# Recurrence gates activated by ScalarE straight from PSUM in the input projection, with their logarithms and scans moved there

## Chip, core and metric

The kernel runs on one core of a Trainium2 chip. The metric is device time in microseconds (us) for one execution of the whole program. The kernel before takes 2365.54 us, the median of three runs (2364.43 to 2369.72).

## What is computed

Two transformer blocks on one sequence of 512 tokens, width 1024, all in float32. The change lies in the first part of the first block, which mixes tokens in two ways from one projection:

```
proj = rmsnorm(h) @ w_in           # 512 x 3592
fq, fk, fv, ff, gq, gf, gi, gg = split(proj)   # widths 512,512,512,8,512,512,512,512
log_f = log_sigmoid(ff + bias)
fox   = softmax(fq fk^T/8 + F[t] - F[s], causal) fv      # F = cumsum(log_f), 8 heads of 64
f  = lb + (1 - lb) * sigmoid(gf);  k = 1 - f;  g = log(f)
q  = silu(gq)
S_t = diag(f_t) S_{t-1} + k_t i_t^T;  rec_t = S_t^T q_t      # 4 heads of 128, in chunks
rec = rmsnorm(rec) * silu(gg)
h  = h + concat(fox, rec) @ w_out
```

The recurrence needs, besides q, k and i, the cumulative sums of g within chunks. After it follow cross attention, a feed-forward part, and the second block; the change touches nothing there.

## The kernel before

Activations lie transposed in SBUF (features on 128 partitions, 512 tokens along the free dimension) unless noted. The program is written by hand for five instruction streams (TensorE, VectorE, ScalarE, GpSimd which the profile calls POOL, and SyncE for the DMAs), which meet through counting semaphores. Each engine works through its own stream in order, so a wait in one stream holds all that stands behind it there.

**Weights.** `plan` cuts every weight matrix into units of 1024 x 256 (1 MB). For each unit SyncE loads `raw`, ScalarE copies it to the rounded high part `wH` (L635, helper `high`), and POOL subtracts to give the low part `wL` (L511, helper `low`). There are two buffers of each. TensorE multiplies high by high, low by high and high by low (L1701 to L1703), so a unit is two blocks of 24 matmuls of 128x512 (feature units), or two blocks of token-major output (token units). `high(n)` waits until unit n - 2 is used up. TensorE waits for both parts of a unit.

**PSUM.** Block b goes to bank b % 4. Before a block TensorE waits until block b - 4 is taken out: `bank_free` looks at `BY_ACT` to see whether that was VectorE's work (semaphore `blk_taken`, counts in `TAKEN`) or ScalarE's (`silu_done`, counts in `SILUS`). In the kernel before only the `ffn_w1` units of the second block are ScalarE's.

**The input projection** has 15 units: 0 to 5 for fq, fk, fv, unit 6 (one block, the eight forget logits), 7 and 8 for gq, 9 and 10 for gf (tile `gk`), 11 and 12 for gi (token units), 13 and 14 for gg. VectorE takes each block from PSUM with a copy (helper `take`, L1084). ScalarE's stream here is `high(n + 1)` for each unit, and at unit 8 the three operations of the forget rows (L750 to L752: Abs, Exp, Ln), after which VectorE forms the cumulative sums `frow` (L1182 to L1184) between the blocks of gk and gi.

**The first attention** (`attention("fox")`) starts when all blocks are taken. It has 8 heads of 4 query blocks, so 32 steps s. TensorE: in step s the scores (L1805) and the causal mask (L1807), the transposes of step s - 3 (L1854), and after a head's last step its eight value matmuls (L1832); once a head, a broadcast of the next head's forget sums (L1796). VectorE: maximum with subtraction (L1112), then the reciprocal and scaling of the step before (L1121, L1122). ScalarE: exponential (L705), the copy of the transposed weights (L724), the broadcast's copy (L694), once per two heads the high part of the output (L730). All depend on each other within a few steps.

Into this chain the kernel before lays the gates of the recurrence. At step 8 ScalarE applies Silu to all of `gq`, Silu to all of `gg` and Sigmoid to all of `gk` (128x2048 each, L710 to L712). From step 10 on VectorE takes one item of `gate_steps` per step: a mask (L1193, L1194), then for each of four heads f and k = 1 - f (L1198, L1199); at step 16 ScalarE takes the logarithms (L716), six steps later VectorE runs the four scans (L1205). The recurrence's own stage begins after the attention on all engines.

A function of ScalarE that is not in the table at hand brings a table load; it appears as ACT_TABLE_LOAD under the line that needs it.

Of the kernel before, what the change touches and what calls it, by code (L numbers as in the profile page):

```python
# [11 lines left out]
ALU = mybir.AluOpType  # L12
ACT = mybir.ActivationFunctionType
# [97 lines left out]
N_UNITS = len(UNITS)  # L111
BLOCK0 = [sum(u[5] for u in UNITS[:n]) for n in range(N_UNITS + 1)]

BY_ACT = [u[0].startswith("ffn_w1") for u in UNITS for _ in range(u[5])]
TAKEN = [sum(not x for x in BY_ACT[:b]) for b in range(len(BY_ACT) + 1)]
SILUS = [sum(x for x in BY_ACT[:b]) for b in range(len(BY_ACT) + 1)]

# [64 lines left out]
def bass_block_pair(nc, a, out):  # L182
# [155 lines left out]
    with ExitStack() as ctx:  # L338
# [25 lines left out]
        f_l, f_rows, f_bc, f_bcs = sem("f_l"), sem("f_rows"), sem("f_bc"), sem("f_bcs")  # L364

        lvl_in = sem("lvl_in")
        h_act, h_fk, h_ln, h_b = sem("h_act"), sem("h_fk"), sem("h_ln"), sem("h_b")
        h_d, h_e, h_q, h_k, h_pl, h_at = sem("h_d"), sem("h_e"), sem("h_q"), sem("h_k"), sem("h_pl"), sem("h_at")
        h_eb, h_qb, h_kd, h_kt, h_kts, h_sp, h_st, h_o, h_os = (
            sem("h_eb"), sem("h_qb"), sem("h_kd"), sem("h_kt"), sem("h_kts"), sem("h_sp"), sem("h_st"), sem("h_o"), sem("h_os"))  # L370
# [246 lines left out]
        def _(act):  # L617
# [63 lines left out]
            def attention(kind):  # L681
                c = ATT[kind]
                ns = c["heads"] * TB
                width = {"fox": None, "cross": M_MEM, "grid": S}[kind]
                for s in range(ns + 7):
                    g = c["step0"] + s
                    if kind == "fox":

                        h = 0 if s == 0 else (s + 2) // 4 if s % 4 == 2 else FOX_H
                        if h < FOX_H:  # L690
                            act.wait_ge(f_bc, h + 1)
                            if h >= 2:
                                act.wait_ge(mx_done, 4 * (h - 1))
                            nc.scalar.activation(fbc[h % 2][:], ps[2 + h % 2][:], ACT.Copy).then_inc(f_bcs, 1)  # L694
                    if s < ns:
                        i = s % TB
                        w = (i + 1) * P if kind == "fox" else width
                        act.wait_ge(mx_done, g + 1)
                        if kind == "fox":
                            src = pr[g % PR_RING][:, 0:w]  # L700
                        else:
                            src = ps[4 + g % 2][:, 0:w]
                            act.wait_ge(tp_done, g - PR_RING + 1)
                        m = g % PR_RING
                        nc.scalar.activation(pr[m][:, 0:w], src, ACT.Exp, bias=nmax[:, m:m + 1],  # L705
                                             accum_out=rsum[:, m:m + 1]).then_inc(ex_done, 1)
                    if kind == "fox" and s == 8:

                        act.wait_ge(blk_taken, TAKEN[BLOCK0[AT["out"][0]]])
                        nc.scalar.activation(gq[:], gq[:], ACT.Silu).then_inc(h_act, 1)  # L710
                        nc.scalar.activation(gg[:], gg[:], ACT.Silu).then_inc(h_act, 1)
                        nc.scalar.activation(gk[:], gk[:], ACT.Sigmoid).then_inc(h_act, 1)  # L712
                    if kind == "fox" and s == 16:
                        for hh in range(HG_H):
                            act.wait_ge(h_fk, hh + 1)
                            nc.scalar.activation(lnf[:, hh, :], lnf[:, hh, :], ACT.Ln).then_inc(h_ln, 1)  # L716
                    t = s - 3
                    if 0 <= t < ns:
                        h, i = t // TB, t % TB
                        nj = (i + 1) if kind == "fox" else width // P  # L720
                        act.wait_ge(tp_done, c["step0"] + t + 1)
                        if i == 0 and h >= 2:
                            act.wait_ge(pv_done, c["pv0"] + c["pvh"] * (h - 1))
                        nc.scalar.activation(pT[h % 2][:, 0:nj, i * P:(i + 1) * P],  # L724
                                             ps[6 + (c["step0"] + t) % 2][:, 0:nj * P].rearrange("p (j t) -> p j t", j=nj),
                                             ACT.Copy).then_inc(pt_done, 1)

                    for o in outputs(kind, s - 5):
                        act.wait_ge(pv_done, c["pv0"] + (o + 1 if kind == "cross" else 2 * o + 2))
                        nc.scalar.activation(uH[:, c["col0"] + o, :], ps[o % 2][:], ACT.Copy).then_inc(op_hi, 1)  # L730
# [13 lines left out]
            nc.scalar.activation(lbt[:, 8:16], lbt[:, 0:8], ACT.Exp).then_inc(setup, 1)  # L744
            for u, n in enumerate(range(*ranges("in"))):
                high(n + 1)
                if u == 8:

                    act.wait_ge(blk_taken, TAKEN[BLOCK0[AT["in"][0]] + 13])
                    chain(nc.scalar.activation(frow[1][:], fz[:], ACT.Abs))  # L750
# [241 lines left out]
        def _(dve):  # L992
# [104 lines left out]
            def attention(kind):  # L1097
# [3 lines left out]
                for s in range(ns + 8):  # L1101
# [15 lines left out]
                    if 1 <= s <= ns:  # L1117
# [2 lines left out]
                        dve.wait_ge(ex_done, g)  # L1120
                        chain(nc.vector.reciprocal(rinv[:, m:m + 1], rsum[:, m:m + 1]))  # L1121
                        nc.vector.tensor_scalar(pr[m][:, 0:w], pr[m][:, 0:w], rinv[:, m:m + 1], None, ALU.mult).then_inc(pn_done, 1)  # L1122
                    if kind == "fox" and s >= 10:
                        next(hgrn_gates, None)
                    for o in outputs(kind, s - 6):
                        low_op(c["q0"] + o, uL[:, c["col0"] + o, :], ps[o % 2][:], uH[:, c["col0"] + o, :])

# [45 lines left out]
            fb = b + 12  # L1173
            dve.wait_ge(blk_done, fb + 1)
            nc.vector.tensor_scalar(fz[:], ps[fb % 4][0:FOX_H, :], fbias[0:FOX_H, :], None, ALU.add).then_inc(blk_taken, 1)
            for j in range(4):
                take(fb + 1 + j, gq[:, j, :], ps[(fb + 1 + j) % 4][:])
            for j in range(4):
                take(fb + 5 + j, gk[:, j, :], ps[(fb + 5 + j) % 4][:])

            dve.wait_ge(f_l, 1)
            chain(nc.vector.tensor_scalar(frow[2][:], fz[:], 0.0, None, ALU.min))  # L1182
            chain(nc.vector.tensor_tensor(frow[2][:], frow[2][:], frow[1][:], ALU.subtract))
            nc.vector.tensor_tensor_scan(frow[0][:], ones[0:FOX_H, 0:1].to_broadcast([FOX_H, S]), frow[2][:], 0.0,  # L1184
                                         ALU.mult, ALU.add).then_inc(f_rows, 1)
            for u in range(2):
                take_tokens(fb + 9 + 2 * u, gi, u * UC)
            for j in range(4):
                take(fb + 13 + j, gg[:, j, :], ps[(fb + 13 + j) % 4][:])


            def gate_steps():
                chain(nc.vector.memset(rmask[:], 1.0))  # L1193
                chain(nc.vector.memset(rmask[:].rearrange("p (c t) -> p c t", c=TB)[:, :, 0:1], 0.0))  # L1194
                yield
                dve.wait_ge(h_act, 3)
                for h in range(HG_H):
                    chain(nc.vector.tensor_scalar(lnf[:, h, :], gk[:, h, :], omlb[:, h:h + 1], lb[:, h:h + 1], ALU.mult, ALU.add))  # L1198
                    nc.vector.tensor_scalar(gk[:, h, :], lnf[:, h, :], -1.0, 1.0, ALU.mult, ALU.add).then_inc(h_fk, 1)  # L1199
                    yield  # L1200
                for _ in range(6):
                    yield
                for h in range(HG_H):
                    dve.wait_ge(h_ln, h + 1)
                    nc.vector.tensor_tensor_scan(gb[:, h, :], rmask[:], lnf[:, h, :], 0.0, ALU.mult, ALU.add).then_inc(h_b, 1)  # L1205
                    yield

            hgrn_gates = gate_steps()
            attention("fox")
            for _ in hgrn_gates:  # L1210
                pass

            levels = [(h, l) for h in range(HG_H) for l in range(len(HG_LEVELS))]

# [473 lines left out]
        def _(pe):  # L1688
# [98 lines left out]
            def attention(kind):  # L1787
                c = ATT[kind]
                ns = c["heads"] * TB
                pe.wait_ge(blk_taken, TAKEN[BLOCK0[AT[{"fox": "out", "cross": "xo", "grid": "ev_out"}[kind]][0]]])  # L1790

                def gates_everywhere(h):

# [441 lines left out]
```

## Time and profile before

| What | Value |
|---|---|
| median of three runs | 2365.54 us (2364.43 to 2369.72) |
| the profiled execution, its own time | 2369.94 us |
| its span, first to last instruction | 2368.2 us |
| TensorE matmuls busy | 2172.1 us, 92% |
| VectorE busy | 1148.0 us, 48% |
| ScalarE busy | 705.6 us, 30% |
| POOL busy | 845.1 us, 36% |
| mean granted TensorE clock | 0.947 |

All rows come from one execution. Times count from the span's start. PE is TensorE, PEld its weight loads, DVE VectorE, ACT ScalarE. The granted clock is a share of 2.4 GHz: 1.00 is full, 0.50 is half. In a timeline, `[6.21 <-ACT pT L724]` means that the engine was idle for 6.21 us before and was released by that instruction. Matmuls are pipelined, so the durations of neighbours overlap. The profiled execution is one, and the three runs spread over 5 us, so a difference of one or two microseconds between two profiles says little.

### The profile page before, as it was taken

Reading aid. Unit: us, or ns where it says so; the run is one execution under the profiler, and the core shown is the slowest. Engines: PE = TensorE matmul, PEld = TensorE weight load, DVE = VectorE, ACT = ScalarE, POOL = GpSimd, SP = SyncE. Lnnn points to the kernel's source line nnn. Section 1 sums busy time; section 2 is a strip of 40 time slices with the busy share of each in tenths; the row PEclk is TensorE's granted clock in tenths of the full one; section 3 lists DMA queues with packets and bytes.
Section 4 is the critical chain, followed back from the end, with each engine's and each line's share of the span. In section 5 each row is a group of like instructions: output and inputs, shape, how many; then the busy total and the mean of one; then the engine's idle time right before and its main releaser. Section 6 shows DMA issues by size and latency. Waiting matters only on the chain.

```text
span 2368.2 us, 26471 instructions
## 1 busy us (share of the span) xinstructions
PE 2172.1 (92%) x10170; PEld 1730.1 (73%) x10170; DVE 1148.0 (48%) x1876; ACT 705.6 (30%) x938; POOL 845.1 (36%) x303
## 2 busy tenths in 40 slices
PE   6998866899989999989988999999899878999998
PEld 4884355787768788877347888888798557888887
DVE  4112597553378888453545676632465554111112
ACT  3124522332331322333433212222233333222221
POOL 2441063362333333423203443334343323434342
PEclk8997868999999999989899999999999989999999
DMA  4330000342245554222004555522222002232322
GB/s 135 96 92 0 1 10 21 105 143 72 90 142 185 177 191 137 89 71 103 0 18 142 178 178 177 193 91 89 89 90 72 1 1 89 89 107 89 106 85 76
DMA packets 220414, 226.12 MB, mean 95 GB/s; under 512 B 3787, under 2 KB 218524, under 8 KB 220188
## 3 DMA queue, kind: packets, MB, share of 16 engines
q1 hardware_dynamic: 220316, 224.78, 29.2%
q8 instruction: 65, 1.06, 0.2%
q14 instruction: 33, 0.27, 0.0%
HBM read 222.67 MB, written 2.10 MB: 95 GB/s over the span
## 4 chain that ended last, share of the span: by engine, by line
PE 79%; DVE 8%; issue 6%; ACT 4%; POOL 1%; DMA 1%; SPq 0%; DVEq 0%; ACTq 0%; POOLq 0%
PE ps L1701 23%; PE ps L1703 22%; PE ps L1702 22%; PE ps L1832 2%; PE ps L1812 1%; DVE adacc L1379 1%; PE ps L1854 1%; PE ps L1916 1%; ACT wH L635 1%; PE ps L1805 1%; PE ps L1768 1%; PE ps L1823 1%; DVE T L1062 1%; DVE uL L1047 1%; DVE hnL L1049 0%
## 5 line engine op out<-in xcount | busy, mean ns | idle before, releaser
L511 POOL TENSOR_TENSOR wL<-raw,wH 128x2048 fp32r<-128x2048 f32 (+2 forms) x161 | 729.8, 4534 | 1274.6 <-ACT wH L635 1259.9
L1701 PE MATMUL ps<-hnH,wH 128*128 128x512 f32 x1336 | 529.5, 396 | 27.1 <-DVE hnL L1049 14.4
L1703 PE MATMUL ps<-hnH,wL 128*128 128x512 f32 x1336 | 524.5, 393 | 0.0
L1702 PE MATMUL ps<-hnL,wH 128*128 128x512 f32 x1336 | 524.0, 392 | 0.0
L635 ACT ACTIVATE wH<-raw 128x2048 fp32r<-128x2048 f32 (+2 forms) x161 | 302.4, 1879 | 651.1 <-PE ps L1703 631.8
L1701 PE MATMUL ps<-uH,wH 128*128 128x512 f32 x864 | 341.3, 395 | 14.2 <-DVE uL L1047 9.7
L1703 PE MATMUL ps<-uH,wL 128*128 128x512 f32 x864 | 338.6, 392 | 0.0
L1702 PE MATMUL ps<-uL,wH 128*128 128x512 f32 x864 | 338.0, 391 | 0.0
L1701 PEld LDWEIGHTS ps<-hnH,wH 128*128 128x128 f32 x1336 | 253.9, 190 | 81.7 <-issue 30.1
L1703 PEld LDWEIGHTS ps<-hnH,wL 128*128 128x128 f32 x1336 | 253.3, 190 | 53.8
L1702 PEld LDWEIGHTS ps<-hnL,wH 128*128 128x128 f32 x1336 | 254.0, 190 | 52.5 <-issue 0.5
L1379 DVE SCALAR_TENSOR_TENSOR adacc<-adaw,small,adacc 128x256 f32<-128x256 f32 x336 | 278.9, 830 | 12.0
L1701 PEld LDWEIGHTS ps<-uH,wH 128*128 128x128 f32 x864 | 163.5, 189 | 49.8 <-issue 13.5
L1703 PEld LDWEIGHTS ps<-uH,wL 128*128 128x128 f32 x864 | 163.2, 189 | 34.5
L1702 PEld LDWEIGHTS ps<-uL,wH 128*128 128x128 f32 x864 | 163.4, 189 | 33.4
L1505 DVE TENSOR_TENSOR T<-ps,R 128x512 f32<-128x512 f32 x44 | 30.4, 691 | 323.7 <-PE ps L1703 323.7
L1094 DVE SCALAR_TENSOR_TENSOR xT<-ps,mod,xT 128x512 f32<-128x512 f32 x64 | 47.5, 750 | 192.5 <-PE ps L1703 192.4
L1701 PE MATMUL ps<-wH,hnH 128*128 128x256 f32 (+1 forms) x416 | 117.8, 283 | 2.9 <-issue 2.9
L1702 PE MATMUL ps<-wL,hnH 128*128 128x256 f32 (+1 forms) x416 | 117.5, 282 | 0.0
L1703 PE MATMUL ps<-wH,hnL 128*128 128x256 f32 (+1 forms) x416 | 117.5, 282 | 0.0
L1408 DVE TENSOR_TENSOR uL<-T,uH 128x512 fp32r<-128x512 f32 x32 | 84.6, 2681 | 21.7 <-ACT uH L834 21.7
L898 ACT ACTIVATE uH<-T 128x512 fp32r<-128x512 f32 x44 | 27.8, 633 | 190.6 <-DVE T L1505 190.6
(331 smaller groups left out, 2506.8 us busy)
## 6 DMA issues: line engine op xcount, KB each, us to landing
raw<-in_ffn_w_dram SPq DMA_DIRECT2D x60, 1024.0 KB, 5.3
adaw<-in_ada_w_dram SPq DMA_DIRECT2D x48, 1024.0 KB, 7.3
raw<-in_w_dram SPq DMA_DIRECT2D x32, 1024.0 KB, 5.4
raw<-in_w_in_dram SPq DMA_DIRECT2D x14, 1024.0 KB, 5.4
raw<-in_od_w_in_dram SPq DMA_DIRECT2D x12, 1024.0 KB, 5.3
raw<-in_w_xkv_dram SPq DMA_DIRECT2D x8, 1024.0 KB, 5.3
raw<-in_ffn_w_dram SPq DMA_DIRECT2D x8, 768.0 KB, 4.2
raw<-in_ev_w_in_dram SPq DMA_DIRECT2D x5, 1024.0 KB, 5.4
```

The lines of the kernel that those rows point to most:

```text
L511: nc.gpsimd.tensor_tensor(wL[n % 2][:, 0:kc, 0:c], raw[n % 2][:, 0:kc, 0:c], wH[n % 2][:, 0:kc, 0:c].bitcast(F32), ALU.subtract).then_inc( ...
L635: nc.scalar.activation(wH[n % 2][:, 0:kc, 0:c], raw[n % 2][:, 0:kc, 0:c], ACT.Copy).then_inc(w_hi, 1)
L898: nc.scalar.activation(uH[:, 2 * p + c, :], T[(q0 + c) % 2][:], ACT.Copy).then_inc(op_hi, 1)
L1047: nc.vector.tensor_tensor(dstL, src, dstH.bitcast(F32), ALU.subtract).then_inc(op_lo, 1)
L1094: nc.vector.scalar_tensor_tensor(out=xT[:, j, :], in0=ps[b % 4][:], scalar=gate(j), in1=xT[:, j, :], op0=ALU.mult, op1=ALU.add).then_inc(b ...
L1379: ins = nc.vector.scalar_tensor_tensor(out=acc, in0=adaw[m % ADA_RING][:, k, :], scalar=condc[:, k:k + 1], in1=acc, op0=ALU.mult, op1=ALU.add)
L1408: nc.vector.tensor_tensor(uL[:, 2 * u + c, :], T[q % 2][:], uH[:, 2 * u + c, :].bitcast(F32), ALU.subtract).then_inc(op_lo, 1)
L1505: nc.vector.tensor_tensor(T[(q0 + c) % 2][:], ps[b % 4][:], R[c][:], ALU.mult).then_inc(blk_taken, 1)
L1701: nc.tensor.matmul(out_ap, wh, xh, start=first, stop=False)
L1702: nc.tensor.matmul(out_ap, wh, xl, start=False, stop=False)
L1703: return nc.tensor.matmul(out_ap, wl, xh, start=False, stop=last)
L1832: ins = nc.tensor.matmul(ps[h // 2 % 2][hp:hp + 64, t0:S], v, pT[h % 2][:, j, t0:S], start=(j == 0), stop=(j == TB - 1))
```

## The change

The blocks of units 7 to 10, 13 and 14 become ScalarE's: as each of the twelve is finished in PSUM, ScalarE applies Silu (gq, gg) or Sigmoid (gk) from the bank into SBUF, in place of VectorE's copy, and counts `silu_done`. In ScalarE's stream the two activations of a unit stand behind `high(n + 1)` of the same unit. The forget rows' three operations move from unit 8 to unit 11, the four logarithms from the attention's step 16 to unit 12. VectorE forms f and k head by head as the blocks of gk are activated, takes the first half of gi, then forms the forget sums, takes the second half of gi, and runs the four scans, all before the attention. The attention's streams lose all of this; TensorE now waits at its start for `silu_done` as well.

```diff
--- before.py
+++ after.py
@@ -111,7 +111,8 @@
 N_UNITS = len(UNITS)
 BLOCK0 = [sum(u[5] for u in UNITS[:n]) for n in range(N_UNITS + 1)]
 
-BY_ACT = [u[0].startswith("ffn_w1") for u in UNITS for _ in range(u[5])]
+GATE_UNITS = (7, 8, 9, 10, 13, 14)
+BY_ACT = [u[0].startswith("ffn_w1") or n in GATE_UNITS for n, u in enumerate(UNITS) for _ in range(u[5])]
 TAKEN = [sum(not x for x in BY_ACT[:b]) for b in range(len(BY_ACT) + 1)]
 SILUS = [sum(x for x in BY_ACT[:b]) for b in range(len(BY_ACT) + 1)]
 
@@ -364,7 +365,7 @@
         f_l, f_rows, f_bc, f_bcs = sem("f_l"), sem("f_rows"), sem("f_bc"), sem("f_bcs")
 
         lvl_in = sem("lvl_in")
-        h_act, h_fk, h_ln, h_b = sem("h_act"), sem("h_fk"), sem("h_ln"), sem("h_b")
+        h_fk, h_ln, h_b = sem("h_fk"), sem("h_ln"), sem("h_b")
         h_d, h_e, h_q, h_k, h_pl, h_at = sem("h_d"), sem("h_e"), sem("h_q"), sem("h_k"), sem("h_pl"), sem("h_at")
         h_eb, h_qb, h_kd, h_kt, h_kts, h_sp, h_st, h_o, h_os = (
             sem("h_eb"), sem("h_qb"), sem("h_kd"), sem("h_kt"), sem("h_kts"), sem("h_sp"), sem("h_st"), sem("h_o"), sem("h_os"))
@@ -704,16 +705,6 @@
                         m = g % PR_RING
                         nc.scalar.activation(pr[m][:, 0:w], src, ACT.Exp, bias=nmax[:, m:m + 1],
                                              accum_out=rsum[:, m:m + 1]).then_inc(ex_done, 1)
-                    if kind == "fox" and s == 8:
-
-                        act.wait_ge(blk_taken, TAKEN[BLOCK0[AT["out"][0]]])
-                        nc.scalar.activation(gq[:], gq[:], ACT.Silu).then_inc(h_act, 1)
-                        nc.scalar.activation(gg[:], gg[:], ACT.Silu).then_inc(h_act, 1)
-                        nc.scalar.activation(gk[:], gk[:], ACT.Sigmoid).then_inc(h_act, 1)
-                    if kind == "fox" and s == 16:
-                        for hh in range(HG_H):
-                            act.wait_ge(h_fk, hh + 1)
-                            nc.scalar.activation(lnf[:, hh, :], lnf[:, hh, :], ACT.Ln).then_inc(h_ln, 1)
                     t = s - 3
                     if 0 <= t < ns:
                         h, i = t // TB, t % TB
@@ -744,7 +735,17 @@
             nc.scalar.activation(lbt[:, 8:16], lbt[:, 0:8], ACT.Exp).then_inc(setup, 1)
             for u, n in enumerate(range(*ranges("in"))):
                 high(n + 1)
-                if u == 8:
+                if u in GATE_UNITS:
+                    dst, func = {7: (gq, ACT.Silu), 9: (gk, ACT.Sigmoid), 13: (gg, ACT.Silu)}[u - (u + 1) % 2]
+                    for c in range(2):
+                        b = BLOCK0[n] + c
+                        act.wait_ge(blk_done, b + 1)
+                        nc.scalar.activation(dst[:, 2 * ((u + 1) % 2) + c, :], ps[b % 4][:], func).then_inc(silu_done, 1)
+                if u == 12:
+                    for hh in range(HG_H):
+                        act.wait_ge(h_fk, hh + 1)
+                        nc.scalar.activation(lnf[:, hh, :], lnf[:, hh, :], ACT.Ln).then_inc(h_ln, 1)
+                if u == 11:
 
                     act.wait_ge(blk_taken, TAKEN[BLOCK0[AT["in"][0]] + 13])
                     chain(nc.scalar.activation(frow[1][:], fz[:], ACT.Abs))
@@ -1120,8 +1121,6 @@
                         dve.wait_ge(ex_done, g)
                         chain(nc.vector.reciprocal(rinv[:, m:m + 1], rsum[:, m:m + 1]))
                         nc.vector.tensor_scalar(pr[m][:, 0:w], pr[m][:, 0:w], rinv[:, m:m + 1], None, ALU.mult).then_inc(pn_done, 1)
-                    if kind == "fox" and s >= 10:
-                        next(hgrn_gates, None)
                     for o in outputs(kind, s - 6):
                         low_op(c["q0"] + o, uL[:, c["col0"] + o, :], ps[o % 2][:], uH[:, c["col0"] + o, :])
 
@@ -1173,42 +1172,24 @@
             fb = b + 12
             dve.wait_ge(blk_done, fb + 1)
             nc.vector.tensor_scalar(fz[:], ps[fb % 4][0:FOX_H, :], fbias[0:FOX_H, :], None, ALU.add).then_inc(blk_taken, 1)
-            for j in range(4):
-                take(fb + 1 + j, gq[:, j, :], ps[(fb + 1 + j) % 4][:])
-            for j in range(4):
-                take(fb + 5 + j, gk[:, j, :], ps[(fb + 5 + j) % 4][:])
-
+            chain(nc.vector.memset(rmask[:], 1.0))
+            chain(nc.vector.memset(rmask[:].rearrange("p (c t) -> p c t", c=TB)[:, :, 0:1], 0.0))
+            for h in range(HG_H):
+                dve.wait_ge(silu_done, SILUS[fb + 5 + h + 1])
+                chain(nc.vector.tensor_scalar(lnf[:, h, :], gk[:, h, :], omlb[:, h:h + 1], lb[:, h:h + 1], ALU.mult, ALU.add))
+                nc.vector.tensor_scalar(gk[:, h, :], lnf[:, h, :], -1.0, 1.0, ALU.mult, ALU.add).then_inc(h_fk, 1)
+            take_tokens(fb + 9, gi, 0)
             dve.wait_ge(f_l, 1)
             chain(nc.vector.tensor_scalar(frow[2][:], fz[:], 0.0, None, ALU.min))
             chain(nc.vector.tensor_tensor(frow[2][:], frow[2][:], frow[1][:], ALU.subtract))
             nc.vector.tensor_tensor_scan(frow[0][:], ones[0:FOX_H, 0:1].to_broadcast([FOX_H, S]), frow[2][:], 0.0,
                                          ALU.mult, ALU.add).then_inc(f_rows, 1)
-            for u in range(2):
-                take_tokens(fb + 9 + 2 * u, gi, u * UC)
-            for j in range(4):
-                take(fb + 13 + j, gg[:, j, :], ps[(fb + 13 + j) % 4][:])
-
-
-            def gate_steps():
-                chain(nc.vector.memset(rmask[:], 1.0))
-                chain(nc.vector.memset(rmask[:].rearrange("p (c t) -> p c t", c=TB)[:, :, 0:1], 0.0))
-                yield
-                dve.wait_ge(h_act, 3)
-                for h in range(HG_H):
-                    chain(nc.vector.tensor_scalar(lnf[:, h, :], gk[:, h, :], omlb[:, h:h + 1], lb[:, h:h + 1], ALU.mult, ALU.add))
-                    nc.vector.tensor_scalar(gk[:, h, :], lnf[:, h, :], -1.0, 1.0, ALU.mult, ALU.add).then_inc(h_fk, 1)
-                    yield
-                for _ in range(6):
-                    yield
-                for h in range(HG_H):
-                    dve.wait_ge(h_ln, h + 1)
-                    nc.vector.tensor_tensor_scan(gb[:, h, :], rmask[:], lnf[:, h, :], 0.0, ALU.mult, ALU.add).then_inc(h_b, 1)
-                    yield
-
-            hgrn_gates = gate_steps()
+            take_tokens(fb + 11, gi, UC)
+            for h in range(HG_H):
+                dve.wait_ge(h_ln, h + 1)
+                nc.vector.tensor_tensor_scan(gb[:, h, :], rmask[:], lnf[:, h, :], 0.0, ALU.mult, ALU.add).then_inc(h_b, 1)
             attention("fox")
-            for _ in hgrn_gates:
-                pass
+            dve.wait_ge(silu_done, SILUS[BLOCK0[AT["out"][0]]])
 
             levels = [(h, l) for h in range(HG_H) for l in range(len(HG_LEVELS))]
 
@@ -1788,6 +1769,8 @@
                 c = ATT[kind]
                 ns = c["heads"] * TB
                 pe.wait_ge(blk_taken, TAKEN[BLOCK0[AT[{"fox": "out", "cross": "xo", "grid": "ev_out"}[kind]][0]]])
+                if kind == "fox":
+                    pe.wait_ge(silu_done, SILUS[BLOCK0[AT["out"][0]]])
 
                 def gates_everywhere(h):
```

## Rows read from the trace of the kernel before

**Rows 1.** The page: the chain that ended last, by line

```profile
PE ps L1701 23%; PE ps L1703 22%; PE ps L1702 22%; PE ps L1832 2%; PE ps L1812 1%; DVE adacc L1379 1%; PE ps L1854 1%; PE ps L1916 1%; ACT wH L635 1%; PE ps L1805 1%; PE ps L1768 1%; PE ps L1823 1%; DVE T L1062 1%; DVE uL L1047 1%; DVE hnL L1049 0%
```

**Rows 2.** Busy time by stretch: us, PE, PEld, DVE, ACT, POOL, clock, DMA share, GB/s

```profile
85.00:198.00 113.00, 111.19 (x647) 98.31 (x646) 16.43 (x24) 21.46 (x14) 45.36 (x11) 1.00 0.28 84
198.00:296.00 98.00, 85.36 (x256) 35.56 (x256) 46.41 (x180) 52.68 (x121) 0.00 (x0) 0.74 0.00 1
```

**Rows 3.** ScalarE groups of the attention: count, busy us, mean ns, idle before

```profile
L705 ACT ACT_TABLE_LOAD x3 | 3.8, 1283 | 0.1
...
L716 ACT ACTIVATE lnf<-lnf 128x512 f32<-128x512 f32 x4 | 2.2, 616 | 0.0
...
L710 ACT ACTIVATE gq<-gq 128x2048 f32<-128x2048 f32 x1 | 1.9, 1910 | 0.0
```

**Rows 4.** Timeline of TensorE, waits for ScalarE: start, duration, [idle before, releaser]

```profile
231.82 1.09 PE L1854 MATMUL ps<-cst,pr 128*128 128x128 f32 x4 [6.21 <-ACT pT L724]
...
254.60 1.08 PE L1854 MATMUL ps<-cst,pr 128*128 128x128 f32 x4 [1.25 <-ACT pT L724]
```

**Rows 5.** Busy time of the attention, cut where the clock changes

```profile
198.30:221.20 22.90, 22.90 (x49) 8.64 (x49) 8.28 (x38) 9.48 (x25) 0.00 (x0) 0.57 0.00 0
221.20:225.20 4.00, 4.00 (x16) 1.93 (x15) 1.93 (x10) 2.50 (x4) 0.00 (x0) 0.93 0.00 0
...
238.90:252.50 13.60, 12.21 (x51) 5.62 (x49) 9.21 (x37) 7.16 (x18) 0.00 (x0) 1.00 0.00 1
...
262.70:266.10 3.40, 3.40 (x15) 1.72 (x15) 1.52 (x9) 1.25 (x4) 0.00 (x0) 1.00 0.00 0
266.10:272.90 6.80, 6.80 (x14) 2.20 (x13) 6.62 (x17) 3.63 (x10) 0.00 (x0) 0.50 0.01 2
272.90:295.90 23.00, 20.07 (x85) 9.48 (x83) 11.65 (x46) 10.66 (x30) 0.00 (x0) 1.00 0.00 0
```

**Rows 6.** Timeline of TensorE: first score matmuls of heads, and value matmuls

```profile
206.29 0.79 PE L1805 MATMUL ps<-fk,fq 64*128 64x128 f32 x2
...
216.76 4.53 PE L1832 MATMUL ps<-pT,fv 128*64 128x512 f32 x8
221.22 0.73 PE L1805 MATMUL ps<-fk,fq 64*128 64x128 f32 x2
...
239.47 0.48 PE L1805 MATMUL ps<-fk,fq 64*128 64x128 f32 x2
...
248.99 0.49 PE L1805 MATMUL ps<-fk,fq 64*128 64x128 f32 x2
...
270.54 3.55 PE L1832 MATMUL ps<-pT,fv 128*64 128x512 f32 x8
274.02 0.49 PE L1805 MATMUL ps<-fk,fq 64*128 64x128 f32 x2
...
282.43 0.49 PE L1805 MATMUL ps<-fk,fq 64*128 64x128 f32 x2
```

**Rows 7.** VectorE groups of the gate steps, 230 to 280 us

```profile
L1205 DVE TENSOR_TENSOR_SCAN gb<-rmask,lnf 128x512 f32<-128x512 f32 x4 | 4.9, 1217 | 0.0
...
L1198 DVE TENSOR_SCALAR lnf<-gk,small 128x512 f32<-128x512 f32 x4 | 2.2, 541 | 0.0
...
L1199 DVE TENSOR_SCALAR gk<-lnf 128x512 f32<-128x512 f32 x4 | 1.7, 427 | 0.1
```

**Rows 8.** ScalarE groups of the whole span: Silu from PSUM in a later stage

```profile
L894 ACT ACTIVATE R<-ps 128x512 f32<-128x512 f32 x44 | 25.9, 598 | 133.5 <-PE ps L1703 133.5
```

**Rows 9.** Timeline of ScalarE, then of POOL: the weights' high and low parts

```profile
141.90 1.92 ACT L635 ACTIVATE wH<-raw 128x2048 fp32r<-128x2048 f32 x1 [8.96 <-PE ps L1703]
152.78 1.91 ACT L635 ACTIVATE wH<-raw 128x2048 fp32r<-128x2048 f32 x1 [8.96 <-PE ps L1703]
...
143.89 4.60 POOL L511 TENSOR_TENSOR wL<-raw,wH 128x2048 fp32r<-128x2048 f32 x1 [6.28 <-ACT wH L635]
154.77 5.35 POOL L511 TENSOR_TENSOR wL<-raw,wH 128x2048 fp32r<-128x2048 f32 x1 [6.28 <-ACT wH L635]
```

## The prediction

> **What bounds the kernel now.** I read the page's chain first: three lines of weight-block matmuls hold 67% of it [rows 1]. Work moved from one helper engine to another can matter only where TensorE waits for it, so the next view is the busy time by stretch around the diff [rows 2]. The input projection, to 198 us, has TensorE at 111 of 113 us and full clock, with VectorE and ScalarE busy for 16 and 21 us. The first attention, 198 to 296 us, has TensorE at 85 of 98 us, a mean clock of 0.74, ScalarE at 53, VectorE at 46 and POOL at 0.
>
> Third, the ScalarE groups of the attention [rows 3], one row for each pattern: Silu on 128x2048 takes 1.91 us (a second Silu and the Sigmoid the same), a logarithm 0.62 us, a table load 1.28 us. Fourth, TensorE's waits for ScalarE there [rows 4]: transposes that wait 6.21 us until 231.82, since ScalarE is at the activations, and 1.25 us until 254.60, at the logarithms. Fifth, the stage cut where the granted clock changes [rows 5]: full (2.4 GHz) for 4.0, 13.6, 3.4 and 23.0 us, half (1.2 GHz) for nearly all the rest, some 54 us.
>
> The clock matters as much as the waits. The first score matmuls of two consecutive heads stand at 206.29 and 221.22, a head at half clock, 14.9 us; later at 274.02 and 282.43, a head at full clock, 8.4 us, one scan in it [rows 6]. The rises at 221.2 and 272.9 lie in or right behind a head's eight value matmuls (from 216.76, from 270.54), and so do the two between them. The falls at 225.2 and 266.1 come with TensorE busy for 4.00 of 4.00 and 3.40 of 3.40 us since the rise [rows 5], in the sparse steps behind such a run; that at 252.5 comes before the second wait begins (254.60 - 1.25 = 253.35).
>
> **The change part by part.** *Activations in the attention, removed.* ScalarE loses three of 1.9 us, four logarithms (2.5 us) and five table loads: one each for Silu, Sigmoid and Ln, two that bring Exp back (L705's third, at the attention's start, stays), 6.4 us [rows 3]. Of these 14.6 us TensorE felt 6.2 + 1.25 us as waits [rows 4].
>
> *VectorE's gate steps in the attention, removed.* Four pairs of 0.54 and 0.43 us and four scans of 1.22 us, 8.8 us [rows 7]. The head from 239.47 to 248.99 ran at full clock with three of the pairs in it and took 9.5 us against 8.4 us [rows 6]: 1.1 us on the path. Two of the scans lie in the half-clock stretch in which TensorE was busy 6.80 of 6.80 us [rows 5]: hidden.
>
> *The clock.* From the first step of head 2 (221.22) to that of head 7 (282.43) are five heads in 61.2 us [rows 6]. Five at the full-clock price are 42.0 us, 19.2 us less. That is the most; it takes in the waits and steps above. But the fall at 225.2 came before ScalarE's absence reached TensorE (231.82 - 6.21 = 225.6) [rows 4, 5], so nothing in the change removes it. It catches the head about half way, and the half clock then lasts into that head's value matmuls, as before. One such spell costs half of a head's difference, (14.9 - 8.4) / 2 = 3.3 us; with a small chance of a second I take 3.5 us (0 and 3 x 3.5 are the ends). The start to 221.2 and the end from 282.43 on hold nothing of the change. **Sum for the attention: 19.2 - 3.5 = 15.7 us.**
>
> The rows thus show falls with a busy engine. The Trainium skill ("TensorE: Matmul & The Clock Gate", section "Why this matters for your kernels") lays drops in mid-kernel to idle gaps between bursts of matmuls; by it no fall would be left once both waits are gone, and the sum would be 19.2 us. The trace disagrees for the falls named.
>
> *Twelve activations from PSUM, added to ScalarE in the projection.* Silu of a 128x512 bank takes 0.60 us [rows 8], in place of a VectorE copy. Each pair is followed on ScalarE by the high part of a coming unit's weights, and that by POOL's low part, for which TensorE waits. Today the high part starts when a unit ends (141.90, 152.78: a unit lasts 10.9 us) and the low part, from 143.89 on, is done after 4.60 us, 6.6 us behind the start: 4.3 us of cover [rows 9]. A unit's second activation comes first now and takes 0.65 us of it. Table loads are issued while ScalarE idles between blocks. Cost nothing; without the cover, 0.65 us for each of six units, 3.9 us.
>
> *The forget gate's three operations* move behind the high part at 152.78, with one more table load: some 4.5 us, ready near 160. VectorE asks for them a unit on, near 165; the row sums are used at 198. The logarithms come behind the next high part and end near 169, the scans run from 176 on. Cost nothing, 20 us of cover. A gate block's PSUM bank is asked for some three blocks, 16 us, after its activation: nothing. SP and POOL keep their order and no DMA is moved.
>
> *VectorE's pairs and scans in the projection* run beside POOL's subtraction; in the attention POOL was idle [rows 2]. The subtraction at 154.77, with the forget rows' sum in its time, took 5.35 instead of 4.60 us [rows 9]. Four scans in a row could add four times that, 3 us, against 4.3 - 0.65 us of cover. 0 to 1 us on the path, 0 taken, as the cover is larger.
>
> *The attention's start.* TensorE waits for a 0.60 us activation of the last bank instead of a copy; ScalarE loads Exp behind its first copy, as now. Between a gain of 0.1 and a loss of 1.3 us (a load in the way); 0 taken, since the load keeps its place.
>
> **Sum against the profiled execution:** 2369.9 - 15.7 = 2354.2 us. That execution is 4.4 us above the median of the three runs. If those 4.4 us lie elsewhere, the new median is 2349.8; if in this attention, 2354.2. I take 2351, nearer to the first, since the stage is only 98 of 2368 us.
>
> **The rivals.** *A, the clock stays up.* No fall after 221.2: 19.2 us, 2350.7 on the profiled basis, 2346 as a median. For it: 23.0 us at full clock at the stage's end [rows 5]. Against: the two falls with a busy engine.
>
> *B, only the waits go.* The clock falls as often as today and the change gives back 6.2 + 1.3 + 1.1 + some 0.3 us for a scan, 8.9 us: 2361.0, or 2356.6 as a median. For it: falls came behind value matmuls without any of the gates' work. Against: heads that follow each other more densely should lose the clock less often.
>
> *C, POOL's weights come late.* With scans and a pair beside it the subtraction outgrows its cover and TensorE waits 1 to 4 us before the last units: 2352 to 2355. For it the 5.35 us row, against it the cover. The Trainium skill ("GPSIMD Engine Reference", Specifications) has POOL's SBUF interface shared with VectorE instructions of two SBUF inputs or in a two-port mode, which speaks against moving these twelve steps here; the row agrees, its size stays inside the cover.
>
> *D, slower: the clock never comes back in this stage.* Five heads at half clock take 5 x 14.9 = 74.5 us for today's 61.2, and the last 13.5 us some 7 more: 20 us slower, 2386 as a median. Each head at half costs 6.5 of the 19.2 us: from three on the gain is gone, from four on it is a loss above 0.2%. Against: each of the four value runs that met half clock brought it back.
>
> *E, no effect:* the removed work lay beside the chain. The 6.21 us wait speaks against it.
>
> **How the numbers follow.** Forecast 0.52, A 0.17, B 0.20, C 0.04, E 0.04, D 0.03. The range goes from A with 3 us for the luck of single runs, 2343, to B with its 4.4 us above, 2361; E, D and a rest of the others lie outside, under 0.2. A measurement of this kernel can tell some 0.2%, 4.7 us, from no change. Faster 0.93, same 0.04, slower 0.03.
>
> **What would show it.** In the changed profile: no table load between the attention's first exponential and its end; no TensorE wait above 2 us for a ScalarE copy there; the stage some 82 us long (79 by A, 89 by B, 118 by D); POOL's subtractions ended 3 us before the unit that needs them, TensorE above 98% busy in the projection; and the first fall of the clock again before 226 us. A projection over 1 us longer makes the second part wrong, a stage of 89 us or more the third.

## The result, and the profile after

The changed kernel takes 2352.26 us (median; 2346.77 to 2355.88, five runs) against 2365.54 us before: a ratio of 0.9937 [0.9925, 0.995], 13.3 us less. A second series of the same kernel, called c_change below, gave 2346.86 us (2346.22 to 2351.37) against 2368.46: 0.9918 [0.9904, 0.9931], 21.6 us less. Of the 8.3 us between the two gains, 5.4 are the changed kernel's and 2.9 those of the kernel before, whose medians differ too. The ten runs together have a median of 2350.2 us, and they spread over 9.7 us, which is itself a finding (below).

I cut each profiled execution at the first broadcast matmul of the attention, at VectorE's first operation of the recurrence behind it, and at the first matmul of the output projection. In us:

| kernel | start and projection | attention | recurrence | rest | span |
|---|---|---|---|---|---|
| before | 198.3 | 97.7 | 114.0 | 1958.2 | 2368.2 |
| changed, first series | 199.5 | 85.9 | 113.9 | 1954.8 | 2354.1 |
| changed, c_change | 198.5 | 77.5 | 114.6 | 1954.4 | 2345.1 |

So 11.8 us of the 14.1 come from the attention in the one profile, and 20.1 of 23.1 in the other. Some 3.5 us come in both from behind the recurrence, where the diff touches nothing. (In the first profile everything from the high part at 58.70 us on, at 57.44 before, is some 1.2 us late; that stands in the set-up.)

The page of the changed kernel, its chain by line, beside [rows 1]; its large terms are where they were:

```profile
PE ps L1682 23%; PE ps L1684 23%; PE ps L1683 23%; PE ps L1815 2%; PE ps L1795 1%; PE ps L1788 1%; PE ps L1837 1%; DVE adacc L1360 1%; PE ps L1899 1%; PE ps L1749 1%; ACT wH L636 1%; PE ps L1806 1%; DVE uL L1048 1%; DVE at L1227 0%; PE ps L2102 0%
```

Busy time by stretch of the changed kernel, first series, columns as in [rows 2] (us, PE, PEld, DVE, ACT, POOL, clock, DMA share, GB/s):

```profile
85.00:199.30 114.30, 112.45 (x658) 99.61 (x656) 23.19 (x26) 35.20 (x34) 47.31 (x11) 1.00 0.27 83
199.30:285.50 86.20, 82.45 (x256) 34.54 (x256) 37.81 (x165) 38.80 (x110) 0.00 (x0) 0.78 0.00 1
```

and the same of c_change:

```profile
85.00:198.40 113.40, 111.47 (x650) 98.59 (x648) 23.19 (x26) 35.29 (x34) 46.34 (x11) 1.00 0.28 84
198.40:276.00 77.60, 73.02 (x256) 31.67 (x256) 37.59 (x164) 38.73 (x110) 0.00 (x0) 0.89 0.00 1
```

ScalarE's 52.7 us in the attention are 38.8 and VectorE's 46.4 are 37.8; what is missing stands in the projection now. TensorE issues the same 256 matmuls. In both profiles it idles less, 12.6 us before, 3.8 and 4.6 now. What differs between the two is the clock, 0.78 and 0.89. The first attention cut where the clock changes, first series, beside [rows 5]:

```profile
221.20:224.80 3.60, 3.60 (x15) 1.68 (x15) 1.84 (x10) 1.01 (x4) 0.00 (x0) 0.97 0.00 0
224.80:231.60 6.80, 6.80 (x14) 2.44 (x14) 2.60 (x11) 3.38 (x10) 0.00 (x0) 0.51 0.00 0
231.60:245.20 13.60, 13.12 (x57) 6.18 (x55) 7.05 (x32) 6.46 (x20) 0.00 (x0) 1.00 0.00 1
245.20:252.00 6.80, 6.80 (x14) 2.31 (x13) 2.34 (x10) 2.80 (x8) 0.00 (x0) 0.50 0.00 0
252.00:255.60 3.60, 3.60 (x17) 1.85 (x16) 1.58 (x9) 1.25 (x4) 0.00 (x0) 0.97 0.00 0
255.60:262.40 6.80, 6.80 (x14) 2.21 (x13) 3.46 (x14) 3.63 (x10) 0.00 (x0) 0.51 0.01 2
262.40:285.40 23.00, 20.02 (x85) 9.47 (x83) 10.58 (x45) 10.70 (x30) 0.00 (x0) 1.00 0.00 0
```

and c_change's:

```profile
198.50:202.20 3.70, 3.69 (x11) 1.60 (x12) 0.59 (x4) 2.37 (x4) 0.00 (x0) 0.99 0.00 0
202.20:219.20 17.00, 17.00 (x35) 6.23 (x35) 7.69 (x35) 7.10 (x21) 0.00 (x0) 0.50 0.00 1
219.20:276.00 56.80, 52.33 (x212) 23.83 (x210) 29.30 (x126) 29.24 (x84) 0.00 (x0) 1.00 0.00 1
```

The same program had three spells at half clock behind the first rise in one execution, and none in the other. All three begin with TensorE at work since the rise: busy for 3.60 of 3.60, 13.12 of 13.60 and 3.60 of 3.60 us.

The waits of [rows 4] are gone. So is a third, of 1.40 us until 246.69, in the head that had three of VectorE's pairs in it (the two operations for f and k). ScalarE loads one table in this stage where it loaded six. TensorE's longest wait for ScalarE there, from the timeline of the first series, is the ordinary one for a head's last exponential:

```profile
281.75 2.37 PE L1815 MATMUL ps<-pT,fv 128*64 128x512 f32 x8 [0.69 <-ACT pT L715]
```

### The profile page after: what moved, and what is told of

It is laid out like the page before. It is cut to its first block, busy times and chain, and to the rows that moved or that the text cites. A ratio compares the mean times of both kernels' runs of the same rounds, so it can differ in the third digit from the quotient of the medians.

```text
span 2354.1 us, 26492 instructions
## 1 busy us (share of the span) xinstructions
PE 2169.4 (92%) x10170; PEld 1730.1 (73%) x10170; DVE 1141.3 (48%) x1864; ACT 705.6 (30%) x946; POOL 845.9 (36%) x303
## 4 chain that ended last, share of the span: by engine, by line
PE 81%; DVE 8%; issue 6%; ACT 2%; POOL 1%; DMA 0%; DVEq 0%; SPq 0%; ACTq 0%; POOLq 0%
PE ps L1682 23%; PE ps L1684 23%; PE ps L1683 23%; PE ps L1815 2%; PE ps L1795 1%; PE ps L1788 1%; PE ps L1837 1%; DVE adacc L1360 1%; PE ps L1899 1%; PE ps L1749 1%; ACT wH L636 1%; PE ps L1806 1%; DVE uL L1048 1%; DVE at L1227 0%; PE ps L2102 0%
```

## The experiments

Ten kernels ran, in three series with their own runs of the kernel before, whose medians are 2368.46, 2367.28 and 2367.68 us; so a difference of one microsecond between kernels of two series says nothing. "Wide" marks those with e3's broadcast. Each kernel has one profile, and a stage's length in one profile holds what the clock did in it. A spell is a stretch at half clock.

**c_change: the same kernel again.**

> The change as it is, again, so that the others of this call have it on the same chip. All theories: 2350 to 2354 us as a median, 11 to 15 us under the kernel before. The stage of the first attention is 86 us long in the change's profile and 98 us in the profile of before; since the times of single runs spread over 9 us, another profile should show another number of stretches at half clock in that stage (the change's first had three after 221 us), and the stage's length should follow it by some 3 us for each.

Measured: 2346.86 us, 3 us below what I expected, with the attention at 77.5 us. Five heads took 42.4 us from one score matmul (220.12) to another (262.55); the forecast's full-clock price was 42.0. In the first series the same five took 50.8 us with three spells: 8.4 us more, 2.8 us for each.

**e1_acts_only: only the twelve activations are moved.** Logarithms, pairs and scans go back into the attention:

```
+    if kind == "fox" and s == 16:
+        for hh in range(HG_H):
+            act.wait_ge(h_fk, hh + 1)
+            nc.scalar.activation(lnf[:, hh, :], lnf[:, hh, :], ACT.Ln).then_inc(h_ln, 1)
...
+    if kind == "fox" and s >= 10:
+        next(hgrn_gates, None)
```

> Of the change only the twelve activations from PSUM are made in the projection; the pairs, the logarithms (step 16) and the scans stay in the attention. Theory that the waits for ScalarE and the clock behind them carry the gain: the 6.2 us wait goes, the 1.25 us wait of the logarithms and the 1.1 us of the pairs stay with their share of the clock, so 7 to 9 us of the 13 us come: about 2357 us. Rival, that VectorE's steps in the chain carry it: no more than 3 us, 2362 or above. Rival, that the Silu wait alone carries everything: 2352, as the change.

Measured: 2358.87 us (2356.49 to 2363.09), ratio 0.9964 [0.9952, 0.9976]; the attention 89.2 us, clock 0.79. TensorE's wait of 6.21 us is gone; one for the logarithms stays, 1.57 us until 245.06, and one beside the scans, 1.59 us until 260.41. Of its own series' 2368.46 us it takes off 9.6; c_change, in the same series, takes off 21.6, and the ten runs of the change 8.7 more than e1. So roughly half of the gain comes with the activations, the rest with the logarithms and VectorE's steps. That rests on the medians. By profiles the rest depends on the clock: e1's has three spells behind the first rise, and its attention is 3.3 us longer than that of the first series, which also has three, and 11.7 us longer than c_change's, which has none.

**e4_left_out: the gates' work stands nowhere.**

```
-    if kind == "fox" and s == 8:
...
-    if kind == "fox" and s == 16:
...
-    hgrn_gates = gate_steps()
+    for h in range(HG_H):
+        nc.vector.memset(gb[:, h, :], 0.0).then_inc(h_b, 1)
```

> The kernel before with the recurrence's gate work left out altogether: no Silu, Sigmoid, logarithms, pairs, mask and scans (the sums are set to zero); the twelve blocks are copied by VectorE as before. If the projection hides all that the change puts there, this is as long as the change, 2350 to 2354 us. If the activations, the held scans (8.9 us for four instead of 4.9) or POOL's longer subtraction cost anything on the path, it is faster than the change by just that: 0.65 us for each gate unit would make 4 us, 2348.

Measured: 2351.91 us (2348.59 to 2352.55), no faster than the change. The stretches of the kernel that leaves the work out, same columns:

```profile
85.00:198.40 113.40, 111.39 (x649) 98.48 (x647) 18.69 (x28) 21.46 (x14) 45.53 (x11) 1.00 0.28 84
...
219.80:240.40 20.60, 19.82 (x81) 9.11 (x80) 10.88 (x49) 10.03 (x30) 0.00 (x0) 1.00 0.00 0
240.40:247.20 6.80, 6.80 (x14) 2.30 (x14) 2.94 (x13) 3.63 (x10) 0.00 (x0) 0.51 0.00 0
247.20:260.80 13.60, 13.12 (x54) 5.93 (x53) 6.90 (x31) 6.08 (x19) 0.00 (x0) 1.00 0.01 1
260.80:267.60 6.80, 6.80 (x15) 2.64 (x15) 2.48 (x10) 3.18 (x10) 0.00 (x0) 0.50 0.00 0
```

Two readings. Until 198.4 us the projection is as long as c_change's, 113.40 us each, though ScalarE has 13.8 us less to do: the moved work costs nothing there. And with none of that work anywhere, the clock still falls twice, with TensorE at work: 83.2 us are c_change's 77.5 and two spells of 2.9. Nothing of the gates is needed for a fall.

**e3_wide_broadcast: the change, and all 128 rows in the broadcast.** Each head's additive term comes from a matmul (two records in the trace) that spreads its row of `frow` over the partitions, with the 8 rows of the heads as contraction. Here the contraction has 128 rows, 120 of them zeros; output, columns and count stay.

```
-nc.tensor.matmul(ps[2 + h % 2][:], ident[0:FOX_H, h:h + 1].to_broadcast([FOX_H, P]), frow[0][:],
+nc.tensor.matmul(ps[2 + h % 2][:], ident[:, h:h + 1].to_broadcast([P, P]), sq[0][:],
...
+chain(nc.vector.memset(sq[0][:], 0.0))
...
+frow = [sq[0][0:FOX_H, :]] + [place(f"frow{i}", [FOX_H, S], F32, o)[0] for i, o in ((1, SQOFF[1]), (2, TOFF[1]))]
```

> The change, with the broadcast of the forget sums made by a matmul over 128 rows (120 of them zero) in place of 8 rows: same columns, same duration, same result. If the granted clock looks at how many rows of the array work, the falls right behind the value matmuls go, the stage runs at full clock from 221 us on and shortens by up to the three spells of the change's profile, 8.8 us: 2343 to 2348 us. If it looks only at whether matmuls stream, nothing changes: 2350 to 2354 us, with falls at the same places.

Measured: 2336.34 us (2336.19 to 2337.74), ratio 0.9869 [0.9854, 0.9884]: the fastest kernel here, 13.8 us below the change's ten runs and 10.5 below c_change, its neighbour in the series. Its attention in one row:

```profile
198.40:267.20 68.80, 64.00 (x256) 29.00 (x256) 37.59 (x164) 38.70 (x109) 0.00 (x0) 1.00 0.00 1
```

That is below the range that I expected, since I had counted only the three spells. There is no fall at all, not even the first one, which in c_change (202.20 to 219.20) held the first two heads at half clock for 17 us. The score matmuls, with 64 rows of contraction, stayed as they were. The broadcast itself takes no longer. From the timelines, at full clock, of the change (first series) and of e3:

```profile
241.77 1.12 PE L1779 MATMUL ps<-frow,cst 8*128 8x512 f32 x2
```

```profile
212.95 1.02 PE L1780 MATMUL ps<-sq,cst 128*128 128x512 f32 x2
```

A small part of the gain is not the clock: five heads took 41.5 us here (212.24 to 253.72) for 42.4 in c_change, all at full clock.

**e7_before_wide: the kernel before, and that broadcast.** e3's edit on the kernel before.

> The kernel before with nothing changed but the broadcast over 128 rows. Its distance to the change with the same broadcast (2336.3 us) is the price of the gate work in the attention with the clock's own falls taken away. Theory: 6.2 + 1.25 us of waits, 1.1 us of pairs, 0.3 to 1 us of scans, and one or two stretches at half clock that the waits themselves bring, 3 us each: 12 to 16 us, so 2348 to 2352 us. Rival, that the waits only trigger falls which the sparse steps would have brought anyway: no half clock behind a wait of 1.25 us or none at all, 9 to 10 us, 2346 us. Rival, that the change's gain came mostly from the clock's luck: under 6 us, 2342 or less.

Measured: 2357.61 us (2356.37 to 2358.14), ratio 0.9961 [0.9947, 0.9974]; attention 87.8 us, 19.0 above e3. My theory ended at 2352: there are three spells where I had allowed for one or two. TensorE's waits, then the first stretches, of this kernel:

```profile
222.58 1.09 PE L1855 MATMUL ps<-cst,pr 128*128 128x128 f32 x4 [6.50 <-ACT pT L724]
...
245.11 0.63 PE L1855 MATMUL ps<-cst,pr 128*128 128x128 f32 x4 [1.76 <-ACT pT L724]
```

```profile
198.30:219.20 20.90, 17.45 (x65) 7.54 (x65) 10.94 (x51) 15.21 (x31) 0.00 (x0) 1.00 0.00 1
219.20:229.60 10.40, 6.78 (x13) 2.56 (x14) 3.29 (x11) 8.03 (x14) 0.00 (x0) 0.51 0.00 0
229.60:246.60 17.00, 13.82 (x58) 6.38 (x56) 10.08 (x40) 10.72 (x24) 0.00 (x0) 1.00 0.00 0
246.60:253.40 6.80, 5.57 (x12) 2.03 (x11) 1.86 (x7) 3.09 (x10) 0.00 (x0) 0.51 0.00 0
```

The clock stays up until the wait; it falls inside it (222.58 - 6.50 = 216.08, the fall at 219.2) and again behind the second. A third fall, at 260.2, lies in a wait of 1.60 us until 260.56, beside a scan. In every profile with the wide broadcast the falls of this stage stand in or behind a wait of TensorE, so the removed waits do pay for clock. But not every wait brings a fall: one of 1.43 us until 237.20 brought none here. The sum: 8.3 us of waits, 1.1 of pairs, 1.2 of scans (e8, below), and half of the 15.4 us that TensorE was busy at half clock (6.78, 5.57 and 3.04) make 18.3 of the 19.0 us.

**e9_acts_only_wide: e1 with it.**

> The change with the wide broadcast, but pairs, logarithms (two table loads) and scans in the attention. Theory: 1.3 us for the wait, 1.1 us for the pairs, 0.3 to 1 us for the scans: 2.7 to 3.5 us above 2336.3 us, so 2339 to 2340, if the clock stays up; 2342 to 2343 if the wait brings a fall. The rest of the distance to the kernel before with the wide broadcast is the Silu and Sigmoid block's.

Measured: 2348.16 us (2342.9 to 2348.83), ratio 0.9914 [0.9899, 0.993]; attention 78.2 us, 9.3 above e3, more than I expected. One of its waits and the spell behind it:

```profile
236.03 0.63 PE L1850 MATMUL ps<-cst,pr 128*128 128x128 f32 x4 [1.75 <-ACT pT L719]
```

```profile
237.60:244.40 6.80, 5.41 (x12) 2.08 (x11) 1.86 (x7) 3.01 (x10) 0.00 (x0) 0.50 0.00 0
```

A second spell follows at 251.2: two, where I had allowed for one. It begins inside a wait that is not the logarithms' but stands beside a scan:

```profile
251.52 3.89 PE L1828 MATMUL ps<-pT,fv 128*64 128x512 f32 x8 [1.60 <-ACT pT L719]
```

The next kernel has the same wait without a fall, so what this second spell hangs on is not shown.

**e8_scans_back_wide: e3, with the four scans back in the attention** (steps 21 to 24; logarithms and pairs stay in the projection; otherwise e1's VectorE edit).

> The change with the wide broadcast, and only the four scans back in the attention (steps 21 to 24). Theory: 0.3 us for each scan that meets a head at full clock, 1.2 us in all: 2337.5 us. Rival, that VectorE is on the chain in every step at full clock: the whole 4 x 1.22 us, 2341 us. Rival, that VectorE has room in every step: 2336.3 us.

Measured: 2342.27 us (2341.31 to 2342.98), ratio 0.9895 [0.988, 0.991]. The attention is 70.07 us for e3's 68.84, 1.2 us for four scans, with no fall in spite of one wait:

```profile
244.25 2.37 PE L1826 MATMUL ps<-pT,fv 128*64 128x512 f32 x8 [1.59 <-ACT pT L715]
```

The time is 4.8 us above my theory; that part lies behind the recurrence, 1958.4 us for 1953.9.

**e6_copies_wide: e3, and a wait for ScalarE that no gate needs.** Three in-place copies of 1.9 us where the activations stood:

```
+if kind == "fox" and s == 8:
+    act.wait_ge(silu_done, SILUS[BLOCK0[AT["out"][0]]])
+    for x in (gq, gg, gk):
+        nc.scalar.activation(x[:], x[:], ACT.Copy).then_inc(h_act, 1)
```

> The change with the wide broadcast and, at step 8 of the attention, three plain copies of 128x2048 in place by ScalarE (they alter no value): 5.7 us of ScalarE with no table load. In the kernel before the block had three table loads more, held ScalarE for 8.1 us up to its next copy for the chain and 9.6 us up to its next exponential, and TensorE waited 6.2 us. Theory: ScalarE's slack is the difference, 1.9 us, so TensorE waits 3.8 us; with a fall of the clock behind it 3 us more: 2340 to 2343 us. Were TensorE's loss due to the table loads alone, 2336 to 2337 us.

Measured: 2346.26 us (2342.97 to 2348.57), ratio 0.9908 [0.9893, 0.9923]. The copies and the wait that they make:

```profile
214.78 1.90 ACT L711 ACTIVATE gq<-gq 128x2048 f32<-128x2048 f32 x1
```

```profile
220.69 0.95 PE L1843 MATMUL ps<-cst,pr 128*128 128x128 f32 x4 [3.66 <-ACT pT L719]
```

The attention is 75.55 us, 6.7 above e3: the wait, 3.7, leaves 3.0 for the one spell (from 220.8), as the theory had it. The time is above its 2343 because the part behind the recurrence is a long one again, 1958.1 us. So neither the wait nor the spell needs a table load or the gates' work.

**e10_scans_scaled_act and e11_wide_scaled_act: the 4 us behind the recurrence.** In the output projection VectorE scales two blocks of memory rows. The kernel before, timeline of VectorE and POOL there:

```profile
423.37 7.39 DVE L1334 TENSOR_SCALAR mtok<-mtok,small 128x1024 f32<-128x1024 f32 x2
...
420.67 9.54 POOL L511 TENSOR_TENSOR wL<-raw,wH 128x2048 fp32r<-128x2048 f32 x2 [35.92 <-ACT wH L635]
```

and c_change's:

```profile
405.47 1.42 DVE L1315 TENSOR_SCALAR mtok<-mtok,small 128x1024 f32<-128x1024 f32 x2
```

Caught beside POOL's subtraction the two take 7.4 us (2.4 and 5.1 in the kernel before), else 1.4. e10 is e8, e11 is e3, each with the scalings on ScalarE:

```
-nc.vector.tensor_scalar(mtok[:, mb, :], mtok[:, mb, :], mstat[:, 2 + mb:3 + mb], None, ALU.mult).then_inc(m_n, 1)
+act.wait_ge(m_inv, 1)
+nc.scalar.activation(mtok[:, mb, :], mtok[:, mb, :], ACT.Copy, scale=mstat[:, 2 + mb:3 + mb]).then_inc(m_n, 1)
```

> The kernel with wide broadcast and scans back in the attention (2342.3 us), whose attention was only 1.2 us longer than without the scans, but whose part behind the recurrence was 4.5 us longer. There the two VectorE scalings of the memory rows (128x1024) took 2.4 and 5.0 us instead of 0.75 us each, beside POOL's subtraction. Here ScalarE does these two. If they are the cause, the part behind the recurrence falls from 1958.4 to about 1954 us and the time to about 2338 us; if they are only beside it, it stays at 2342 us.

> The change with the wide broadcast (2336.3 us, part behind the recurrence 1953.9 us, scalings of 0.75 us), with the two scalings on ScalarE. They were not held there, so there is nothing to gain: 2336 to 2338 us, the last for ScalarE's two operations ahead of the next high part. If the held scalings cost time in every execution, 2333 us.

Measured: e10 2338.02 us (2337.47, 2338.01, 2338.03 and 2342.5), ratio 0.9872 [0.9856, 0.9889], 4.3 us below e8. e11 2337.3 us (2336.86 to 2337.99), ratio 0.9871 [0.9855, 0.9888], no gain on e3. That looks as expected, but does not settle it. The profiled execution of e10 is the one of 2342.5 us, with a rest of 1958.5 us and no scaling on VectorE; and two profiles had both scalings caught in a short rest: the change's first, 1.8 and 5.1 us in 1954.8, and e1's, 1.7 and 5.1 us in 1953.8. So held scalings are not what makes the rest long. In e8's profile TensorE waits 3.2 us for a high part in the output projection, until 398.74, and then the clock falls:

```profile
399.80:403.20 3.40, 3.40 (x10) 2.68 (x9) 3.40 (x1) 0.00 (x0) 3.40 (x1) 0.52 0.92 307
```

The kernel before, e6, e8 and the profiled execution of e10 have the long rest, 1958.1 to 1958.5 us, the other eight profiles 1953.8 to 1956.0. All four long ones have this spell of 3.4 us with TensorE busy throughout (from 426.6, 405.2, 399.6 and 399.2), right behind a wait for a high part of 2.1 to 3.2 us; none of the eight has it, though the change's first profile has a wait of 2.20 us there. The spell accounts for 1.7 us of some 4. What brings it stays open.

## Why the prediction was right

Forecast 2351.0 us, between 2343 and 2361; measured 2352.26, all ten runs together 2350.2.

**The waits and the work** were as forecast: 6.21 and 1.25 us of wait became 0.69 at most. The small prices held: the head with the pairs took 9.3 us in e9 for 8.4 in e3, where I had put 1.1 us for them; scans in an attention at full clock cost 1.2 us for four (e8), where B put 0.3 us for one. (Three of the scans began in the busy half-clock stretch of the kernel before, not two as I wrote: 266.48, 269.31 and 271.76. No term changes by it.)

**The projection costs nothing:** e4 shows it. The mechanism feared as C is real, only smaller than its cover. The changed kernel, first series, VectorE's scans and POOL's subtractions:

```profile
177.62 8.93 DVE L1190 TENSOR_TENSOR_SCAN gb<-rmask,lnf 128x512 f32<-128x512 f32 x4
```

```profile
167.54 5.35 POOL L512 TENSOR_TENSOR wL<-raw,wH 128x2048 fp32r<-128x2048 f32 x1 [6.47 <-ACT wH L636]
179.07 5.28 POOL L512 TENSOR_TENSOR wL<-raw,wH 128x2048 fp32r<-128x2048 f32 x1 [6.17 <-ACT wH L636]
190.39 4.60 POOL L512 TENSOR_TENSOR wL<-raw,wH 128x2048 fp32r<-128x2048 f32 x1 [6.05 <-ACT wH L636]
```

and the third of the four scans by itself:

```profile
179.87 5.56 DVE L1190 TENSOR_TENSOR_SCAN gb<-rmask,lnf 128x512 f32<-128x512 f32 x1
```

Four scans take 8.9 us for the 4.9 of [rows 7], the subtraction beside them 5.28 for 4.60; at 184.35 it is done, some 3.5 us before its unit begins. The four are not slowed alike. Three take 1.2 us each; the third, which starts at 179.87 with the subtraction under way, takes 5.56 and ends 1.1 us behind it, so it was held until the subtraction was done. I had bounded the loss at 3 us, four times one scan's; it is 0.7, since the subtraction met only one scan that was already running, at its start, and the held one cost VectorE time that nothing waited for. The Trainium skill ("GPSIMD Engine Reference", Specifications) has the two engines share their SBUF interface for VectorE instructions with two SBUF inputs; these rows agree. A unit's second activation takes 0.49 us from the cover, from its start to that of the high part, where I had put 0.65; ScalarE's timeline of the changed kernel:

```profile
153.98 0.60 ACT L743 ACTIVATE gk<-ps 128x512 f32<-128x512 f32 x1 [4.84 <-PE ps L1684]
154.47 1.91 ACT L636 ACTIVATE wH<-raw 128x2048 fp32r<-128x2048 f32 x1
```

**The clock.** The full-clock price of five heads, 42.0 us, was met with 42.4. The price of a spell, 3.3 us, was 2.8 to 3.0. What I had wrong is their number: "One such spell", with a small chance of a second. The profiles show none and three, and e4 two. With three the attention gains 11.8 us, with none 20.1; no profile has the one spell of my sum. My 15.7 stands between, so that the median of executions which differ by spells came out near 2351 is in part luck. The argument behind the one spell, that the fall at 225.2 precedes every wait and so must come back, held in the first series (224.8) and failed in c_change. Rival A, to which I gave 0.17, is what c_change's attention shows, 77.5 us for its 79; its median of 2346 was c_change's. B's time (2356.6) was nearly reached by single runs (2355.88), though not by its mechanism: no wait is left, only spells.

I also held that falls with a busy engine belong to the "sparse steps" and took them as given. e3 shows what they hang on: with the same count and columns of matmuls none is left. The Trainium skill ("TensorE: Matmul & The Clock Gate", section "Why this matters for your kernels") lays drops to idle gaps between bursts; in the kernels with the 8-row broadcast the trace disagrees (three spells in the first series, and no gap above 0.69 us). With the wide one it agrees for the long waits, 6.50 us in e7 and 3.66 us in e6, each with a spell, and for e3, which has neither. Waits of 1.4 to 1.8 us went both ways: those of 1.75 and 1.60 us in e9 have spells, one of 1.42 us there and e8's of 1.59 us have none.

**The 4.4 us** by which the profiled execution lay above the median: 3.4 to 3.8 us of them are in the rest, outside the attention, as I had leaned. The change touches nothing there, and e10's one program has executions 4.5 us apart, the long one with a rest of 1958.5 us. Whether the kernel before has the long rest more often than the changed one, and so whether a part of the medians' difference is this, no run here shows.

## What to carry to other kernels

Moving work off a helper engine pays twice where the wait that it made also dropped TensorE's clock: e7 to e3 is 21 us for some 11 us of waits and steps. Where a stage's clock falls although TensorE is busy, look for matmuls with few rows of contraction in it and try to fill them up with zeros: it cost nothing measurable and gave another 14 us here. The four runs of e3 spread over 1.5 us, the ten of the change over 9.7; where waits of TensorE were left in (e6, e9) the spread stayed near 6. Before counting spells in one profile, take a second profile of the same kernel.

## What the runs showed of the hardware that I had not expected

In this attention the granted clock depended on what the matmuls feed to the array, not only on whether TensorE was at work. Sixteen broadcast matmuls, 1.1 us a pair with 8 rows and 1.0 us with 128, were all that differed on TensorE: 77.5 or 85.9 us of attention against 68.8, clock 0.89 or 0.78 against 1.00. The kernel before with the same edit (e7) has lost its first fall too. The Trainium skill ("TensorE: Matmul & The Clock Gate", section "Why this matters for your kernels") has a matmul of few rows take the time of a full one, and these two rows agree. Whether it is the rows of the matmul or of its weight load that counts wasn't tried apart, nor the zeros against other data, nor the 0.2 us by which each head is shorter with the wide broadcast.

With the 8-row broadcasts the clock of one program differed from execution to execution: no spell, or three, behind the first rise. And a VectorE operation that meets a POOL subtraction under way can be held until it ends: a scan took 5.56 us for 1.2, a scaling of 128x1024 5.1 us for 0.75.
